# Fox keys by row tile as the first projection, another order of the first loads and splits, in a hybrid encoder step

## The reference

```
h   = rms_norm(x, norm_g[0])
qa, ka, va, fa, xb, yb, qc, kc, vc = split(h @ w_in)      # 256 256 256 4 512 512 256 256 256 columns
logf  = log_sigmoid(fa + b_forget)
o_fox = fox_attention(qa, [cache, ka], [cache, va], [cache, logf])
o_lru = rglru_block(xb, yb, ...)                            # conv, two gates, linear scan, times gelu(yb)
o_band = band_attention(qc, [cache, kc], [cache, vc], rel_bias)
x = x + rms_norm(concat(o_fox, o_lru, o_band) @ w_out, norm_g[1])
gate, val = split(rms_norm(x, norm_g[2]) @ w_up)
y = x + rms_norm((gelu(causal_conv(gate)) * val) @ w_down, norm_g[3])
```

## Time and profile before

| | |
|---|---|
| median of the runs | 1504.38 us (1501.41 to 1505.44, 3 runs) |
| the profiled execution | 1503.04 us |
| its span in the profile | 1501.3 us |
| mean granted TensorE clock | 0.989 |
| busy: PE, DVE, ACT, POOL | 96%, 48%, 31%, 6% of the span |
| PE's share of the chain that ended last | 93% |

### The profile page before, as it was taken

One profiled execution on the slowest core, in us unless ns is written; L12 is line 12 of the kernel. 1 busy time (PEld: TensorE's weight loads), 2 busy tenths in 40 slices (PEclk: granted clock), 3 DMA queues, 4 the chain that ended last, 5 costly groups with the idle time before them and its releaser, 6 DMA issues.

```text
span 1501.3 us, 20856 instructions
## 1 busy us (share of the span) xinstructions
PE 1443.9 (96%) x8598; PEld 1310.3 (87%) x8598; DVE 715.2 (48%) x1196; ACT 465.1 (31%) x679; POOL 90.9 (6%) x129
## 2 busy tenths in 40 slices
PE   6999999989998999999999999999999999999994
PEld 6999988956776889999999999999999999999983
DVE  6433640167676555544444444353535353535346
ACT  6353341166566434312121212121212121212123
POOL 3000002122000011000000000000000000000006
PEclk9999999999999999999999999999999999999997
DMA  6210222225304233211111111011101010102033
GB/s 212 85 29 29 82 88 95 74 81 183 126 11 155 86 104 114 57 48 44 41 48 36 53 30 55 29 56 28 56 28 56 28 56 28 56 28 70 0 126 132
DMA packets 80006, 102.89 MB, mean 69 GB/s; under 512 B 3592, under 2 KB 63237, under 8 KB 79806
## 3 DMA queue, kind: packets, MB, share of 16 engines
q1 hardware_dynamic: 71744, 73.43, 15.7%
q0 software_dynamic: 8208, 28.69, 5.5%
HBM read 85.52 MB, written 16.58 MB: 68 GB/s over the span
## 4 chain that ended last, share of the span: by engine, by line
PE 93%; DVE 3%; ACT 2%; DMA 1%; issue 0%; POOL 0%; SPq 0%; ACTq 0%; DVEq 0%
PE PS L1436 50%; PE PS L1764 19%; PE PS L1505 7%; PE PS L1731 7%; PE PS L1426 4%; PE PS L1572 2%; PE PS L1665 2%; PE PS L1511 1%; DVE f_acc L1409 1%; PE PS L1595 1%; DVE act_lo L1018 0%; PE PS L1680 0%; DVE f_acc L1382 0%; DMA gains<-in_norm_g 0%; ACT w_hi L751 0%
## 5 line engine op out<-in xcount | busy, mean ns | idle before, releaser
L1436 PE MATMUL PS<-act_hi,w_hi 128*128 128x384 f32 x1152 | 208.4, 334 | 0.0
L1436 PE MATMUL PS<-act_lo,w_hi 128*128 128x384 f32 x1152 | 207.9, 334 | 0.0
L1436 PE MATMUL PS<-act_hi,w_lo 128*128 128x384 f32 x1152 | 207.9, 334 | 0.0
L1436 PEld LDWEIGHTS PS<-act_hi,w_hi 128*128 128x128 f32 x1152 | 200.8, 188 | 0.9
L1436 PEld LDWEIGHTS PS<-act_lo,w_hi 128*128 128x128 f32 x1152 | 200.4, 188 | 0.0
L1436 PEld LDWEIGHTS PS<-act_hi,w_lo 128*128 128x128 f32 x1152 | 200.4, 188 | 0.0
L1382 DVE TENSOR_TENSOR f_acc<-f_acc,PS 128x512 f32<-128x512 f32 x216 | 145.7, 687 | 79.7 <-PE PS L1764 79.6
L1764 PE MATMUL PS<-w_hi,f_hi 128*128 128x512 f32 x432 | 169.3, 392 | 4.8 <-ACT ffn_rows L999 4.8
L1764 PE MATMUL PS<-w_hi,f_lo 128*128 128x512 f32 x432 | 168.8, 391 | 0.0
L1764 PE MATMUL PS<-w_lo,f_hi 128*128 128x512 f32 x432 | 168.8, 391 | 0.0
L921 ACT ACTIVATE w_hi<-raw 128x1024 fp32r<-128x1024 f32 x72 | 72.3, 1051 | 224.9 <-PE PS L1764 219.4
(11 more groups left out here) (326 smaller groups left out, 1953.0 us busy)
## 6 DMA issues: line engine op xcount, KB each, us to landing
raw<-in_w_up SPq DMA_DIRECT2D x48, 512.0 KB, 4.6
raw<-in_w_down SPq DMA_DIRECT2D x24, 512.0 KB, 3.9
raw<-in_w_in SPq DMA_DIRECT2D x18, 512.0 KB, 4.7
x_scratch<-x POOLq DMA_DIRECT2D x9, 512.0 KB, 5.3
x_back<-x_scratch SPq DMA_DIRECT2D x1, 4608.0 KB, 14.3
x_in<-in_x_prompt SPq DMA_DIRECT2D x8, 512.0 KB, 5.3
raw<-in_w_out SPq DMA_DIRECT2D x8, 512.0 KB, 3.7
x_res<-in_x_prompt SPq DMA_DIRECT2D x8, 512.0 KB, 4.4
```

Of the source, the lines that this page charges most:

```text
L1436: last = pe.matmul(PS[0:width, banks + c, 0:CW], w(wp, k), acts[ap][:, k, c * CW:(c + 1) * CW], start=(n == 0 and k == 0), stop=(n == 2 an ...
```

## The change

Unit 0 becomes the fox keys, and the first product is made tile by tile: `fk_tile(t)` on PE makes 24 matmuls of 256 columns for row tile t into bank t % 4, as soon as that tile's low part is there, with the transposes of tile t + 2 behind it. ACT evacuates each piece alone (`take_fk`, 128x256) into `stage`, three iterations of the norm later. `first_output` is gone; all x outputs are now made whole, after the nine pieces and the channel transposes. SP's first loads go x tile 0, norm gains, weight half 0, x tile 1, weight half 1, x tile 2; two more weight halves (unit 1) are loaded among the x tiles and split in iterations 5 and 6. POOL waits for the third scaled tile before it issues the channel loads and all that follows on it. Among DVE's scans the splits move: units 5 and 6 behind the first scan, then 7, 8 and 9 behind the others. The gate pairs follow the outputs y 0, y 3, fox values 2 and band values 1, where they followed y 0, y 3, fox keys 2 and fox values 2.

```diff
-UNITS = [("x", C_X), ("x", C_X + 256), ("y", C_Y), ("y", C_Y + 256), ("fk", C_FK), ("fv", C_FV),
+UNITS = [("fk", C_FK), ("x", C_X), ("x", C_X + 256), ("y", C_Y), ("y", C_Y + 256), ("fv", C_FV),
...
-GATES_AFTER = [("y", 2, 0), ("y", 3, 3), ("fk", 4, 2), ("fv", 5, 2)]
+GATES_AFTER = [("y", 3, 0), ("y", 4, 3), ("fv", 5, 2), ("bv", 7, 1)]
...
-        FIRST_SPLITS = (2, 3)
+        FIRST_SPLITS, SECOND_SPLITS = (0, 1), (5, 6)
+        NFK = NT // 3
+        def wait_fk_used(eng, t):
+            j, c = divmod(t, 3)
+            if c < 2:
+                eng.wait_ge(fk_used, 2 * j + c + 1)
+            else:
+                eng.wait_ge(out_used, j + 1)
...
-            load_in(0)
-            load_in(1)
-            for t in range(3, NT):
-                sp.wait_ge(y_ready, t - 2)
-                sp.dma_start(x_in[:, t % 3, :], rows_of(xp, xs, t)).then_inc(x_loaded[t % 3], 16)
-            for r in range(2, 2 * NU):
+            for t in range(1, NT):
+                if t < 3:
+                    load_in(t - 1)
+                if t in SECOND_SPLITS:
+                    load_in(2 + SECOND_SPLITS.index(t))
+                load_x(t)
+            for r in range(4, 2 * NU):
                 load_in(r)
...
             step(pool.memset(chan_rows[:, :, :], 0.0))
+            pool.wait_ge(y_ready, 3)
...
+            def take_fk(t):
+                j, c = divmod(t, 3)
+                if j == 2 and c == 0:
+                    act.wait_ge(stage_stored[0], 16 * stores_until(0, 0))
+                if c < 2:
+                    act.wait_ge(fk_done, 2 * j + c + 1)
+                else:
+                    act.wait_ge(out_done, j + 1)
+                act.activation(stage[:, j % 2, c, :], PS[:, t % 4, 0:DH], ACT.Copy)\
+                   .then_inc(fk_used if c < 2 else out_used, 1)
...
                 if t in FIRST_SPLITS:
                     split_unit_half(0, FIRST_SPLITS.index(t))
+                if t in SECOND_SPLITS:
+                    split_unit_half(1, SECOND_SPLITS.index(t))
+                if t >= 3:
+                    take_fk(t - 3)
             norm_hi(NT - 1)
+            for t in range(NT - 3, NT):
+                take_fk(t)
...
-            for u in range(1, 3):
-                split_unit(u)
+            split_unit(2)
...
             for j in range(LT):
                 lru_scan(j)
                 if j < LT - 1:
-                    split_unit(5 + j)
+                    for u in ((5, 6), (7,), (8,))[j]:
+                        split_unit(u)
                     lru_conv(j + 1)
-            for u in range(8, NU):
-                split_unit(u)
+            split_unit(9)
...
-            def first_output(j, c, last):
+            def fk_tile(t):
                 pe.wait_ge(w_lo_ready, 2)
-                pe.wait_ge(lo_ready, 3 * (c + 1))
+                pe.wait_ge(lo_ready, t + 1)
+                if t >= 4:
+                    wait_fk_used(pe, t - 4)
                 w0 = [unit_of(w, 0) for w in (w_hi_all, w_lo_all)]
...
+                for m, (ap, wp) in enumerate(((0, 0), (0, 1), (1, 0))):
+                    for k in range(KD):
+                        last = pe.matmul(bank_cols(t % 4, DH), acts[ap][:, k, t * P:(t + 1) * P], w0[wp][:, k, :],
+                                         start=(m == 0 and k == 0), stop=(m == 2 and k == KD - 1))
+                last.then_inc(fk_done if t % 3 < 2 else out_done, 1)
+            turn_x(0)
+            turn_x(1)
+            for t in range(NT):
+                fk_tile(t)
+                if t + 2 < NT:
+                    turn_x(t + 2)
```

More of the change, by code:

```diff
@@ L98, in projection_outputs @@
     for u, (kind, _) in enumerate(UNITS):
-        first = {"x": 2 * u, "y": 2 * (u - 2)}.get(kind, 0)
+        first = {"x": 2 * (u - 1), "y": 2 * (u - 3)}.get(kind, 0)
         if kind != "bk":
@@ L396, in encoder_step @@
         conv_ready = sem("conv_ready")
+        fk_done = sem("fk_done")
+        fk_used = sem("fk_used")
         decay_ready = sem("decay_ready")
@@ L511, in _, with load_x @@
         def _(sp):
[L513 to L517, removed]
+            def load_x(t):
+                if t >= 3:
+                    sp.wait_ge(y_ready, t - 2)
+                sp.dma_start(x_in[:, t % 3, :], rows_of(xp, xs, t)).then_inc(x_loaded[t % 3], 16)
+            load_x(0)
+            sp.dma_start(gains[:, 0, :], i["norm_g"][0, 0:1, :].to_broadcast([P, D])).then_inc(gain_loaded, 16)
             def load_half(r, dst, src):
@@ L775, in split_unit @@
                     split_unit_half(u, half)
-            for u in range(1, 3):
-                split_unit(u)
-            staged, pending = 0, []
+            split_unit(2)
+            staged, pending = NFK, []
             for n, (kind, u, j) in enumerate(OUTS):
                 banks = PS[:, 3 * (n % 2):3 * (n % 2) + 3, :]
-                if kind == "x":
+                if n < NFK:
+                    pass
+                elif kind == "x":
                     act.wait_ge(out_done, n + 1)
@@ L1072, in lru_conv @@
                 x = mix[:, MIX_OF_X[j], :]
-                dve.wait_ge(out_used, OUTS.index(("x", j // 2, j)) + 1)
+                dve.wait_ge(out_used, OUTS.index(("x", 1 + j // 2, j)) + 1)
                 dve.memset(xpad[:, 0:LH], 0.0)
@@ L1103, in lru_scan @@
                 y = mix[:, 2 + j, :]
-                dve.wait_ge(out_used, OUTS.index(("y", 2 + j // 2, j)) + 1)
+                dve.wait_ge(out_used, OUTS.index(("y", 3 + j // 2, j)) + 1)
                 dve.tensor_tensor(y[:, 0:SEQ], y[:, 0:SEQ], xconv[:, 0:SEQ], ALU.mult)
@@ L1484, in _ @@
             for n, (kind, u, j) in enumerate(OUTS):
-                if n < 2:
+                if n < NFK:
                     continue
                 b0 = 3 * (n % 2)
-                if n >= 2:
-                    pe.wait_ge(out_used, n - 1)
+                if n == NFK:
+                    wait_fk_used(pe, 7)
+                pe.wait_ge(out_used, n - 1)
                 if u is not None and u not in seen:
```

19 lines of the change are left out of this document (1 added, 18 removed).

## The result

| | before | changed kernel |
|---|---|---|
| median of the runs, taken together | 1502.89 us (1500.39 to 1505.44, 4 runs) | 1492.74 us (1492.68 to 1494.36, 4 runs) |
| ratio, 95% interval | | 0.9929 [0.9915, 0.9943] |
| the profiled execution, its span | 1503.04, 1501.3 us | 1494.36, 1492.6 us |

Faster by 0.7%, beyond what a measurement can tell from no change. Measured twice more, the changed kernel took 1492.88 and 1493.55 beside 1502.02 (15 runs) and 1502.38 (9 runs) of before: a gain of 9 us.

What follows compares the result with a forecast made beforehand. TensorE holds 93% of the chain, so only its idle time can go. 14.7 start + 26.2 pieces + 6.1 transposes + 0.7 channel rows + 1.7 clock = 49.4 against 56.8: gain 7.4, median 1496.3 us, range 1492.5 to 1501.0.

Steps and rivals of the forecast that it cites:

- The start: PE's first fox key piece begins at 14.7 us against 20.02 before; best 14.4, worst 16.6.
- The loop: Nine fox key pieces: per row tile PE needs 2.91 plus 0.87 for transposes, 3.78 us, without waits; bad end 2.4.
- The clock: PE's low clock level reaching into the first fox key piece costs 0.85 to 2.9 us; 1.7 taken.
- The sum to the first x output: Start, pieces, transposes, channel rows and low clock put fox keys done at 49.4 us against 56.8: gain 7.4.
- What follows keeps it: After the fox keys, later splits, scans and gate pairs stay covered, so the 7.4 us gain is not lost.
- the narrowest place: ACT held by unit 4's splits until about 83 us, while PE first needs ACT at 87: 3 to 4 us spare.
- The same length from there to the end: Attention starts 7 us earlier and the time from its start to the program's end is unchanged.
- halfway between the two: Median placed between the profiled execution and the shown runs' median, 1.3 above it: 1495.6 becomes 1496.3 us.
- The row-tile pacing: In the fox key loop ACT or DVE come late, PE waits 0.4 us at eight tiles; gain 4.0, chance 0.13.
- The low clock through the loop: All nine pieces and seven transpose groups run at the low clock: 1526 us, slower; chance 0.05.
- later wait: At unit 4's split or the second convolution PE waits 3 to 5 us once; gain 3, about 1500.5; chance 0.08.
- the rule of the Trainium skill: An engine cycling PSUM banks with short idles, as in the new loop, can swing between clock levels and lose to re-warming.

Runs made afterwards that it cites:

- The run whose first piece has no low clock: Changed kernel plus identity transposes on idle PE, 22 ahead of and 34 behind row tile 0's transposes, 8 behind row tile 1's: 1491.89 us, ratio 0.9930.
- The run that forced stops: Changed kernel with four transpose groups instead of two ahead of the first fox key piece, and four ahead in the loop: 1522.69 us, ratio 1.0136.

## Why the prediction was right and where it was wrong

Direction, mechanism and places were right; the time is 3.6 us lower than forecast (1492.74 against 1496.3; 3.4 and 2.7 in the two repetitions), at the low edge of the range.

- **The start.** 14.7 forecast, 14.62 found, by the path that was worked out: row tile 1 landed at 9.28 (9.2) and bound it with the two subtractions on DVE. The worst end, 16.6, put the whole 1.9 us of a later weight half on top of 14.7; by the prediction's own terms it is 12.8 + 1.06 + 1.22 = 15.1, so the range was too wide on that side.
- **The loop.** Forecast 3.78 to a tile with no wait; found 2.87 + 0.87 = 3.74 and none. Nine pieces are 25.8, not 26.2. The evacuation, an estimate of 0.4 without a row behind it, took 0.38. The assumption that mattered stood in one sentence, that ACT's evacuation of piece t-3 finds its work done; the run with four transpose groups shows how near its failure lies, at 30 us.
- **The clock.** Forecast 1.7 as the middle of 0.85 and 2.9. The first piece took 3.95 against 2.87: 1.08. It is not a constant: from start to start, first and second piece lie 0.82 further apart than later ones in this trace, and 1.87 in the third one (14.82 to 20.43, less 3.74). The term fell into its bounds, but which end comes out differs between executions of one program, so the sum could not have known. The run whose first piece has no low clock gained 0.9 to 1.7 by the medians.
- **The sum to the first x output.** 49.4 forecast, 48.29 found: clock 0.6, pieces 0.35, start 0.1. Gain 8.5 instead of 7.4; at the attention's start 8.4 and 8.5 in two traces, 7.1 in the third (299.5).
- **What follows keeps it.** Right. At the narrowest place ACT was done with the split at 82.4 (83 forecast) and PE ran through 86 without a wait; the pairs still pay 0.7 three times. "The same length from there to the end" was wrong by up to 2.5 us: the attention took 166.0 before, and 165.6, 165.6 and 163.5 in the three traces after, with the places where the clock falls. The sum had no term for it. The one kept trace of before does not tell whether such differences are the change's or those of single executions.
- **The step that failed** is the one from the profiled execution to the median: "halfway between the two", which put 0.7 on top of 1495.6 because three runs had a median 1.3 above the profiled one. In the changed kernel's own runs the median lies 1.6 below the profiled execution (1492.74 and 1494.36). In before too: the medians of 15, 9 and 9 further runs are 1502.0, 1502.0 and 1502.4, some 0.9 below the profiled execution's 1503.04. Of the 3.6 us this step is 2.3; three runs were taken for the centre of a scatter of 5 us. The sum is the other 1.2: it gave 1495.6 for the profiled execution, which took 1494.36, a gain of 8.7 instead of 7.4. Its mis-sized term is the clock, 1.7 where this trace has 1.08. The term that it put at nothing, the attention, was 0.4 there; in the third trace it was 2.5, with a gain of only 7.1 ahead of it, so what the attention adds to the medians stays open. The low end, 1492.5, allowed for too little when sum, scatter and clock all go one way.
- **The rivals.** The row-tile pacing did not occur: 3.75 between starts, no wait. The low clock through the loop did not: by the lengths the pieces ran at the high level from the second eight matmuls on, in the third trace from within the third eight on. The run that forced stops had it in part, with some 10 us of slow clock beside 16.8 of stops. No later wait took anything. Of the rule of the Trainium skill in the prediction (the page and section named above): a loop over four banks with a wait at each piece kept the high level (8 matmuls in 1.12 to 1.20 us from 16.49 on) and PE did not stop; by the trace the rule decides nothing for the new loop.

## What to carry to other kernels

In this kernel it paid to put first a product that can be cut by row tile, and to let the loads serve its first tile; the load order alone gained nothing (1.0006), the change without it 5.6 of 9 us. Before you put an evacuation into another engine's loop, follow the ring: evacuation, next input's work, next transposes, next piece; two iterations of distance more or less were 26 us here. Where PE idles ahead of its first product, idle transposes up to that product bought about 1 us, and those that left a stop of 2.14 us ahead of its transposes bought nothing.

## What the hardware did that was not expected

- The same program leaves the low clock at different points of the same piece: the first eight matmuls took 1.9 to 2.1 us in all traces of the changed kernel, the next eight 1.12 in two and 1.91 in the third.
- In the attention the granted clock falls in some executions and not in others, at places that differ (0.57 over 304 to 311 us in one trace, 1.00 in another of the same program), and its length varies from 163.3 us (the run with the old load order) to 169.0. Stops of the same lengths, 1.28 us at most, were followed by a fall in one trace and by none in the other. A difference of 1 or 2 us in this kernel can be that alone.
- Raising the clock early did not keep it: it fell again after a stop of 2.14 us, and the first piece ran wholly at the low level, which without the idle transposes only its first third did in two traces (in the third one the first two thirds and part of the last).
- The granted clock in the profile reads 1.00 from the start of the program, also where matmuls take double (2.04 against 1.20). Only after a first fall does the record show the low level (0.50 over 14 to 20 us in the run with 34 idle transposes, at lengths of 2.07 and 1.91): at the start, go by the lengths.
